# Splitting units of 768 tokens as 384 + 384 columns in place of 512 + 256

## The reference

```python
D_MODEL, SEQ, CTX_LEN, DEPTH, D_FF, D_IN = 1024, 512, 256, 2, 2816, 2304

def swiglu(y, w_in, w_out):
    a, gt = jnp.split(y @ w_in, 2, axis=-1)
    return (jax.nn.silu(a) * gt) @ w_out
...
    xl = xl + 0.5 * ml[2] * swiglu(modulate_in(xl, g[0], ml[0], ml[1]), f_in[0], f_out[0])
    xc = xc + 0.5 * mc[2] * swiglu(modulate_in(xc, g[0], mc[0], mc[1]), f_in[0], f_out[0])
    ol, oc = token_mixer(...)            # y @ w_in, mixers, ... @ w_out
    xl = xl + ml[5] * ol
    xl = xl + 0.5 * ml[8] * swiglu(modulate_in(xl, g[2], ml[6], ml[7]), f_in[1], f_out[1])
    if need_ctx:
        xc = xc + mc[5] * oc
        xc = xc + 0.5 * mc[8] * swiglu(...)
```

## Time and profile before

| what | value |
|---|---|
| median of 3 runs | 3049.46 us (3040.86, 3049.46, 3057.99) |
| profiled execution | 3050.23 us |
| its span, first to last instruction | 3048.5 us |
| TensorE matmul busy | 94% of the span |
| VectorE, ScalarE busy | 56%, 28% |
| mean granted TensorE clock | 0.959 of full speed |

### The profile page before, as it was taken

One profiled execution on the slowest core, in us unless ns is written; L12 is line 12 of the kernel. 1 busy time (PEld: TensorE's weight loads), 2 busy tenths in 40 slices (PEclk: granted clock), 3 DMA queues, 4 the chain that ended last, 5 costly groups with the idle time before them and its releaser, 6 DMA issues.

```text
span 3048.5 us, 39841 instructions
## 1 busy us (share of the span) xinstructions
PE 2874.7 (94%) x14770; PEld 2340.1 (77%) x14770; DVE 1718.3 (56%) x2840; ACT 856.6 (28%) x1147; POOL 292.2 (10%) x279
## 2 busy tenths in 40 slices
PE   6999999999779999999999899999998979999998
PEld 5888888877543578888888788888876744678887
DVE  7676676669673356766676772222247664443334
ACT  3221122141363332211221422112232264432222
POOL 1000000024322110000000100000004232000000
PEclk8999999999877999999999999999998979999999
DMA  5333333321220013333333232111212220123232
GB/s 201 117 117 124 111 117 139 103 77 55 56 59 7 21 49 117 117 122 107 123 118 117 76 110 70 62 55 63 74 50 84 74 66 7 55 81 101 91 99 84
DMA packets 63374, 264.94 MB, mean 87 GB/s; under 512 B 8880, under 2 KB 11824, under 8 KB 53680
## 3 DMA queue, kind: packets, MB, share of 16 engines
q1 hardware_dynamic: 50608, 180.17, 18.0%
q0 software_dynamic: 11520, 75.11, 7.6%
q10 hardware_dynamic: 1152, 8.39, 0.7%
HBM read 252.89 MB, written 2.10 MB: 84 GB/s over the span
## 4 chain that ended last, share of the span: by engine, by line
PE 83%; DVE 10%; ACT 4%; issue 2%; DMA 1%; POOL 0%; ACTq 0%; SPq 0%; DVEq 0%
PE ps L1431 74%; PE ps L1670 2%; DVE conv_acc L1184 2%; PE ps L1597 2%; PE ps L1625 1%; PE ps L1605 1%; DVE w_lo L934 1%; DVE rstd L987 1%; DVE nmax L1289 1%; ACT e_sb L846 1%; DMA x<-in_xT 1%; ACT probs_t L860 1%; DVE mod_start_acc L1366 1%; DVE y_hi L1023 0%; DVE sq L1011 0%
## 5 line engine op out<-in xcount | busy, mean ns | idle before, releaser
L1431 PE MATMUL ps<-y_hi,w_hi 128*128 128x512 f32 (+1 forms) x3184 | 912.5, 350 | 65.3 <-DVE y_lo L1015 31.2
L1431 PE MATMUL ps<-y_lo,w_hi 128*128 128x512 f32 (+1 forms) x3184 | 907.8, 349 | 0.0
L1431 PE MATMUL ps<-y_hi,w_lo 128*128 128x512 f32 (+1 forms) x3184 | 900.6, 346 | 0.0
L1431 PEld LDWEIGHTS ps<-y_hi,w_hi 128*128 128x128 f32 x3184 | 519.9, 191 | 164.5 <-issue 35.8
L626 ACT ACTIVATE w_hi<-w_raw 128x1024 fp32r<-128x1024 f32 (+1 forms) x290 | 326.6, 1128 | 1063.9 <-PE ps L1431 1063.9
L1431 PEld LDWEIGHTS ps<-y_lo,w_hi 128*128 128x128 f32 x3184 | 517.1, 190 | 75.9
L1431 PEld LDWEIGHTS ps<-y_hi,w_lo 128*128 128x128 f32 x3184 | 515.0, 190 | 77.7 <-issue 0.2
L934 DVE TENSOR_TENSOR w_lo<-w_raw,w_hi 128x1024 fp32r<-128x1024 f32 (+1 forms) x290 | 384.8, 1327 | 322.3 <-ACT w_hi L626 320.0
L949 DVE SCALAR_TENSOR_TENSOR mod_acc<-mod_raw,cact,mod_acc 128x256 f32<-128x256 f32 x896 | 360.2, 479 | 0.0
L1431 PE MATMUL ps<-h_lo,w_hi 128*128 128x512 f32 (+1 forms) x1254 | 356.8, 344 | 0.0
L1431 PE MATMUL ps<-h_hi,w_hi 128*128 128x512 f32 (+1 forms) x1254 | 356.3, 344 | 0.0
(11 more groups left out here) (162 smaller groups left out, 2033.8 us busy)
## 6 DMA issues: line engine op xcount, KB each, us to landing
w_raw<-in_w_up SPq DMA_DIRECT2D x176, 512.0 KB, 3.5
mod_raw<-in_w_mod POOLq DMA_DIRECT2D x64, 1024.0 KB, 5.1
w_raw<-in_w_down SPq DMA_DIRECT2D x64, 704.0 KB, 4.1
w_raw<-in_w_in SPq DMA_DIRECT2D x36, 512.0 KB, 3.5
mod_start<-in_w_mod ACTq DMA_DIRECT2D x8, 1024.0 KB, 22.0
w_raw<-in_w_out SPq DMA_DIRECT2D x16, 512.0 KB, 3.5
stack<-qk_hi SPq DMA_DIRECT2D x48, 96.0 KB, 2.1
band<-in_rpb POOLq DMA_DIRECT2D x16, 224.0 KB, 6.6
```

Source lines behind the costliest of these rows:

```text
L1431: mm = pe.matmul(slot[s][:, at:at + b - a], w[s][:, k, :], r[:, k, a:b], start=(k == 0 and n == 0), stop=(k == kc - 1 and n == 2))
```

## The change

The units of 768 tokens, but for the first pair behind a norm and the last pair ahead of one, are worked as columns 0 to 383 and 384 to 767. The first range goes to the first bank of the slot and the second to the start of its second bank, so the result lies in PSUM as two pieces of 384 with 128 unused columns between them. ScalarE and VectorE read it with a pattern of two pieces, or flat where the pair is one behind a norm (`is_flat`). The update of `x` takes three instructions in place of two, because the latent columns now lie in both banks: 384 latent, 128 latent, 256 context. The order of the work, the semaphores, the transfers and the number of matmuls and weight loads stay.

```diff
+EVEN = TOK // 2
...
+    def even_spans(tokens):
+        return ((0, EVEN, 0), (EVEN, TOK, LAT)) if tokens == TOK else ((0, LAT, 0),)
+
+    def of_unit(s, tokens, flat):
+        if flat or tokens < TOK:
+            return slot[s][:, 0:tokens]
+        return slot[s].rearrange("p (b c) -> p b c", b=2)[:, :, 0:EVEN]
+
+    def like_unit(tile, tokens, flat):
+        return tile if flat or tokens < TOK else tile.rearrange("p (b c) -> p b c", b=2)
+
+    def is_flat(p, i):
+        return p.after_norm and isinstance(i, int) and i == 0
...
-                    act.activation(act_buf[:, 0:n], slot[0][:, 0:n], ACT.Silu).then_inc(sems["slot_free0"], 1)
+                    act.activation(like_unit(act_buf[:, 0:n], n, is_flat(p, i)), of_unit(0, n, is_flat(p, i)), ACT.Silu).then_inc(sems["slot_free0"], 1)
...
-                        act.activation(z[:, 2 * i + s, 0:tokens], slot[s][:, 0:tokens], func).then_inc(sems[slot_free[s]], 1)
+                        unit = z[:, bass.ds(2 * i + s, 1), 0:tokens].rearrange("p u t -> p (u t)")
+                        act.activation(like_unit(unit, tokens, is_flat(p, i)), of_unit(s, tokens, is_flat(p, i)), func).then_inc(sems[slot_free[s]], 1)
...
-                    dve.tensor_tensor(hid_buf[:, 0:n], act_buf[:, 0:n], slot[1][:, 0:n], ALU.mult).then_inc(sems["slot_free1"], 1)
+                    flat = is_flat(p, i)
+                    dve.tensor_tensor(like_unit(hid_buf[:, 0:n], n, flat), like_unit(act_buf[:, 0:n], n, flat), of_unit(1, n, flat),
+                                      ALU.mult).then_inc(sems["slot_free1"], 1)
...
-                        for k, (lo, hi) in kinds(n):
-                            ins = dve.scalar_tensor_tensor(x[:, 2 * i + s, lo:hi], slot[s][:, lo:hi],
+                        for k, lo, hi, at in ((0, 0, EVEN, 0), (0, EVEN, LAT, LAT), (1, LAT, TOK, 2 * LAT - EVEN)) if n == TOK else ((0, 0, LAT, 0),):
+                            ins = dve.scalar_tensor_tensor(x[:, 2 * i + s, lo:hi], slot[s][:, at:at + hi - lo],
                                                            gates[:, k, bass.ds(2 * i + s, 1)], x[:, 2 * i + s, lo:hi],
                                                            ALU.mult, ALU.add)
...
-                                mm = product(s, k, p.kc, rhs_hi, rhs_lo, [(a, b, a) for a, b in spans(tokens)])
+                                mm = product(s, k, p.kc, rhs_hi, rhs_lo, even_spans(tokens))
```

## The result

The changed kernel takes 3030.24 us (median of 5 runs, 3028.46 to 3031.24) against 3047.75 us (5 runs, 3040.86 to 3057.99). The ratio is 0.9933 with a 95% interval of 0.9911 to 0.9956, so it is 0.7% faster. The profiled execution took 3028.46 us, its span is 3026.8 us, 21.7 less than before.

A forecast was written before the change was run, and what follows sets the result against it. TensorE's pace, 83% of the chain that ended last, was taken to bound the kernel. The sum was 3050.2 - 21 us for slow pairs + 0 for side costs = 3029 us, with a range of 3022 to 3062.

The forecast's parts named there:

- Two paces, and that the slow one goes: TensorE's 512 + 256 pairs take 346.7 or 353.3 ns; equal lengths keep the quick pace, saving 6.6 ns per slow pair.
- the 21 of the sum: From the first mix_out to the second layer's mix_in, 3230 slow pairs each save 6.6 ns: 21 us.
- 384 columns at 173.3 ns: Each 384-column matmul on TensorE starts 173.3 ns after the last, a pair taking 346.7 ns.
- the line I read it from: Straight line through the 256- and 512-column matmul spacings, 120.0 and 226.7 ns, giving 384 columns 160.0 + 13.3 ns.
- rival 2: Equal matmuls on TensorE fall into a slow rhythm of their own, 180 ns each: 3097 us; chance 0.12.
- What weakened it: Stretches of one length stay in one bank and use each weight block once in a row; the changed pairs do neither.
- rival 1: Double weight loads, bank change or a clock phase, not unequal lengths, set TensorE's pace and stay: 3050 us; chance 0.34.
- The weight load without slack: Loads of 107 ns by rule have no slack behind 256 columns; behind 384 they have 53 ns of room.
- Unequal neighbours as the cause: Slow 353.3 ns pairs occur where 512 and 256 columns alternate; stretches of one length run at 346.7 ns.
- The update of x and the reads in pieces at 0: VectorE's third update instruction hides behind 5.0 us waits for TensorE; two-piece reads cost at most 0.2 us: both counted 0.
- The term of 9.6 us: The third instruction of VectorE's x update adds 0.20 us per unit over 48 units: 9.6 us if not hidden.
- The spread: Runs of the kernel before, 3041 to 3058 us, differ in how many stretches are slow, between 3029 and 3063.

The follow-up runs named there:

- range_outer: Kernel before with 512 + 256 columns, but each unit works its 512 columns over all chunks, then its 256; 3033.57 us, ratio 0.9944.
- range_outer_416: 416 + 352 columns touching at the bank boundary, but each unit works its 416 columns over all chunks, then its 352; 3047.84 us, ratio 1.001.
- two other even kernels: 384 + 384 columns touching at the bank boundary, with the update of x in two instructions (3030.82 us) or five (3030.8 us).

## Why the prediction was right

Forecast 3029 us, measured 3030.24; forecast 0.7% less, 21 us, measured 0.67%.

- **Two paces, and that the slow one goes.** Shown. Loops behind the first mixer run at 16.89 us, no slow stretch is left, and the lead of 21.8 us by the start of the last loop, 1.1 of it from elsewhere, is the 21 of the sum.
- **384 columns at 173.3 ns.** Right by the number, 1.04 us for six. But the line I read it from does not hold in general, nor does the constant of 13.3 ns for each matmul: 352 columns among their like take 158.3 or 166.7 ns and not 160.0, and 392 + 376 and 416 + 352 take 352 to 353 a pair. The line is no lower bound either. I named "both neighbours in length are clean" as the evidence against rival 2. It was worth less than I gave it: had 384 been like 392, rival 2 would have come true in mild form, near 353 ns a pair in all stretches and a time like that of 392 + 376, 28 us longer at a like clock. That 384 is a clean length was luck as far as my rows went.
- **What weakened it.** The double load of the same weights and the change of bank stay in the changed kernel, which is quick throughout. Neither is enough to bring the slow pace. That is rival 1 for these two. Its third form, a phase of the clock, is not tested by itself, but whatever is drawn there leaves the even split alone: its 23 runs lie at 3028 to 3033 and 3018 to 3022 us.
- **The weight load without slack.** I left open whether the loads behind 256 columns slip. As the cause it is out: in range_outer 256-column matmuls, each with its load, follow each other at the quick pace, and 416 + 352 leaves the load 40 ns more room than 512 + 256 and is slow throughout.
- **Unequal neighbours as the cause.** For 512 and 256 shown from both sides, by the even split and by range_outer. That equal neighbours suffice at any length is refuted by range_outer_416, which is slow. Why neighbours matter stays open.
- **The update of x and the reads in pieces at 0.** Shown from both sides: two instructions or five give 3031 too. The term of 9.6 us was over-sized, since the third piece adds 0.13 us and not 0.20, and it is hidden. My row for reads in pieces, 677 ns, was of 16 groups that lie side by side, with no gap between them, and so no evidence; the 954 and 813 ns of the changed kernel are.
- **The spread.** Runs from 3029 to 3063 by the draw of slow stretches: that the stretches differ between executions is shown by the second profile of before. I had missed the second draw, 10 us by the clock in the mixer. The 3041 us that I read as fewer slow stretches may as well have been that.
- **Luck in the last digit.** All five runs of the changed kernel have the lower clock; in the two other even kernels 4 of 18 have the higher one and take 3019 to 3022 us. The median of the kernel before lay between 3045.85 and 3052.25 us in the later comparisons.

Open is what in a length makes it clean. Lengths of 256, 384 and 512 are clean among their like, 352 and 416 are not. In turn, 384 + 384 is quick in all three profiles, 448 + 320, 512 + 256 and 256 + 512 know both paces, and 480 + 288, 504 + 264, 416 + 352 and 392 + 376, which aren't multiples of 64 columns, have a steady excess of 2 to 6 ns a pair. This fits a grid of starts on which multiples of 64 columns can lie well, but no run shows the grid itself.

## What to carry to other kernels

Where a loop of matmuls is tight, read its pace from the distance between starts in several stretches and in more than one run, since busy time does not tell 347 from 353 ns. Compare runs at a like mean clock. If the work of a unit needs two matmuls, try equal lengths of a size measured to be clean, or one length over all chunks and then the other. Don't take a length in between from a line: sixteen columns of difference cost the whole gain.

## What the runs showed that I had not expected

The same program has two paces, 346.7 and 353.3 ns for 768 columns at the full clock, and it keeps one for hundreds of microseconds. The changes shown here stand behind a wait for weights or a small matmul; most of these change nothing. Each matmul of 256, 384 or 512 columns carries 13.3 ns beside its columns among its like, while 352 columns carry 11.6 or 20. At a like clock 392 + 376 columns cost 28 us more than 384 + 384. Extra work of 0.38 us per unit on VectorE cost nothing at all.
